# Constant products on an idle TensorE, and column sums spread among output tiles, in a two-block attention and Hyena kernel

## The reference, cut to what matters

```
def adaln_params(cond, w, b):
    mod = jax.nn.silu(cond) @ w + b
    return jnp.split(mod[..., None, :], 6, axis=-1)
...
    x = x + merged @ w_out                     # end of the first block
    x = rms_norm(x, norm_final)
...
    sh1, sc1, g1, sh2, sc2, g2 = adaln_params(c, mod_w, mod_b)
    h = modulate(rmsnorm(x, norm_g[0]), sh1, sc1)
    x = x + g1 * hyena_mix(h, ...)
    x = x + g2 * conv_ffn(modulate(rmsnorm(x, norm_g[1]), sh2, sc2), ...)
    return rmsnorm(x, final_g)
```

## Time and profile before

| | us |
|---|---|
| median of 3 runs | 1089.21 |
| lowest, highest | 1088.16, 1089.78 |
| the profiled execution | 1089.59 |
| its span, first to last instruction | 1087.8 |
| TensorE busy in the span | 1050.8 (97%) |
| VectorE, ScalarE, GpSimd busy | 666.7, 421.2, 543.9 |
| mean granted TensorE clock | 0.988 |

### The profile page before, as it was taken

How to read it: one execution, slowest core, us unless ns; L and a number is a source line. 1 busy time by engine, 2 the same in 40 slices (tenths; PEclk the granted TensorE clock), 3 DMA queues, 4 the chain that set the end, 5 groups by cost and what they waited for, 6 DMA issues and landing times.

```text
span 1087.8 us, 13471 instructions
## 1 busy us (share of the span) xinstructions
PE 1050.8 (97%) x4970; PEld 866.0 (80%) x4970; DVE 666.7 (61%) x1003; ACT 421.2 (39%) x691; POOL 543.9 (50%) x403
## 2 busy tenths in 40 slices
PE   6999998999899999999999999989999999999996
PEld 5889886877777888778888888868888888888885
DVE  5663667775478864966588864467656665620503
ACT  6223656574455243564344333333223322321222
POOL 1688789987000045343344346435546554663541
PEclk9999999999899999989999999999999999999999
DMA  6446354341344842230222223222232223222322
GB/s 250 159 164 226 123 189 168 99 152 44 143 160 176 347 172 67 95 116 14 104 77 78 79 78 155 78 97 78 97 136 77 77 96 136 77 78 99 134 78 77
DMA packets 18567, 131.92 MB, mean 121 GB/s; under 512 B 2369, under 2 KB 2769, under 8 KB 11986
## 3 DMA queue, kind: packets, MB, share of 16 engines
q1 hardware_dynamic: 8784, 92.62, 22.7%
q0 software_dynamic: 6560, 27.27, 7.4%
q10 hardware_dynamic: 3170, 11.30, 2.7%
HBM read 124.89 MB, written 6.29 MB: 121 GB/s over the span
## 4 chain that ended last, share of the span: by engine, by line
PE 85%; DVE 9%; ACT 3%; issue 1%; POOL 1%; DMA 1%; SPq 0%; POOLq 0%; ACTq 0%; DVEq 0%
PE bank L497 73%; PE bank L488 6%; PE bank L503 2%; PE bank L727 1%; PE bank L733 1%; DVE arena L2261 1%; DVE bank L2264 1%; DMA x_sb<-x_in 1%; ACT ring_parts L1143 1%; DVE arena L2101 1%; DVE arena L2319 0%; DVE arena L2104 0%; DVE arena L2317 0%; PE bank L722 0%; ACT arena L1143 0%
## 5 line engine op out<-in xcount | busy, mean ns | idle before, releaser
L1660 POOL TENSOR_TENSOR ring_parts<-ring,ring_parts 128x1024 fp32r<-128x1024 f32 x104 | 253.0, 2437 | 289.2 <-ACT ring_parts L1143 286.9
L1143 ACT ACTIVATE ring_parts<-ring 128x1024 fp32r<-128x1024 f32 (+2 forms) x163 | 168.7, 1042 | 471.4 <-PE bank L497 293.2
L497 PE MATMUL bank<-hT_parts,ring_parts 128*128 128x512 f32 x1344 | 341.9, 396 | 1.3 <-ACT hT_parts L1457 1.3
L497 PEld LDWEIGHTS bank<-hT_parts,ring_parts 128*128 128x128 f32 x1344 | 251.7, 190 | 55.9 <-ACT hT_parts L1457 3.0
L497 PE MATMUL bank<-ring_parts,arena_parts 128*128 128x512 f32 (+1 forms) x736 | 172.5, 387 | 1.5 <-DVE arena L2319 0.8
L497 PE MATMUL bank<-ring_parts,hT_parts 128*128 128x512 f32 (+1 forms) x672 | 171.7, 383 | 0.7 <-POOL ring_parts L1660 0.6
L497 PEld LDWEIGHTS bank<-ring_parts,arena_parts 128*128 128x128 f32 x736 | 136.5, 188 | 29.6 <-DVE arena L2319 1.3
L497 PE MATMUL bank<-arena_parts,ring_parts 128*128 128x512 f32 x592 | 147.8, 391 | 0.3 <-DVE arena_parts L2203 0.3
L497 PEld LDWEIGHTS bank<-ring_parts,hT_parts 128*128 128x128 f32 x672 | 123.8, 190 | 22.9 <-POOL ring_parts L1660 1.0
L2417 DVE SCALAR_TENSOR_TENSOR arena<-bank,small,arena 128x441 f32<-128x441 f32 (+2 forms) x176 | 122.3, 695 | 24.6 <-DVE arena L2412 1.9
L497 PEld LDWEIGHTS bank<-arena_parts,ring_parts 128*128 128x128 f32 x592 | 111.1, 188 | 25.5 <-DVE arena_parts L2203 2.1
(11 more groups left out here) (228 smaller groups left out, 1078.7 us busy)
## 6 DMA issues: line engine op xcount, KB each, us to landing
ring<-weights_in SPq DMA_DIRECT2D x39, 2048.0 KB, 7.9
arena<-mod_w_in POOLq DMA_DIRECT2D x32, 512.0 KB, 4.1
arena<-mod_w_in POOLq DMA_DIRECT2D x8, 1024.0 KB, 5.0
x_sb<-x_in SPq DMA_DIRECT2D x4, 512.0 KB, 5.6
ring<-weights_in SPq DMA_DIRECT2D x4, 512.0 KB, 8.5
mod_spill<-mod_part POOLq DMA_DIRECT2D x16, 128.0 KB, 2.1
x_sb<-x_in ACTq DMA_DIRECT2D x4, 512.0 KB, 12.1
arena<-mod_spill ACTq DMA_DIRECT2D x1, 2048.0 KB, 10.4
```

The costliest lines, as they stand in the source:

```text
L497: ins = nc.tensor.matmul(out, l, r, start=start and n == 0, stop=stop and n == len(passes) - 1)
L1143: return nc.scalar.activation(out, in_, ACT.Copy)
L1660: return nc.gpsimd.tensor_tensor(part(low), low, part(high), ALU.subtract)
```

## The change

`keep_running` is a plain fp32 product of the identity with the first n columns of `small`, whose result nobody reads. It is issued three times before the first token tile and once before the third; in the third norm after the turns of tiles 1 and 2 (512 columns each, in bank 0, after a wait for the reader of that bank) and once with 256 columns after the last turn of k = 1. `modulation(j)` now makes 4 column sums and runs eight times among the output and filter tiles; the gate products have a function of their own, and its last two use banks 4 and 5. VectorE's `modulation()` stands before `norm_x2(2)` instead of at the end, and ScalarE's `modg_copy(2)` after `square_x1(3)`.

```diff
+        MODG_BANK = (2, 2, 4, 5)
...
+            def keep_running(b, n=512):
+                nc.tensor.matmul(bank[b][:, 0:n], ident, small[:, 0:n], start=True, stop=True)
+
             pe.wait_ge(sem("small_in"), 16)
+            for _ in range(3):
+                keep_running(7)
             for m in range(TT):
+                if m == 2:
+                    keep_running(7)
                 pe.wait_ge(sem("n1_scaled"), m + 1)
...
-                for c in range(j * KD, (j + 1) * KD):
+                for c in range(4 * j, 4 * j + 4):
                     ins = nc.tensor.matmul(bank[3][:, c:c + 1], mod_sum(c), st(ONE), start=True, stop=True)
-                ins.then_inc(sem("modc_done"), 1)
-                take(2, "modg_out", j + 1)
-                nc.tensor.matmul(bank[2], ones_sq, mod_g[:, j // 2, (j % 2) * 512:(j % 2) * 512 + 512],
+                if j % 2:
+                    ins.then_inc(sem("modc_done"), 1)
+
+            def gate_rows(j):
+                b = MODG_BANK[j]
+                take(b, "modg_out", j + 1)
+                nc.tensor.matmul(bank[b], ones_sq, mod_g[:, j // 2, (j % 2) * 512:(j % 2) * 512 + 512],
                                  start=True, stop=True).then_inc(sem("modg_done"), 1)
...
             modulation(0)
+            gate_rows(0)
+            modulation(1)
             wo_tile(0)
+            modulation(2)
             wo_tile(1)
-            modulation(1)
+            gate_rows(1)
+            modulation(3)
             filter_tile(0)
             wo_tile(2)
+            modulation(4)
             filter_tile(1)
             wo_tile(3)
+            modulation(5)
             filter_tile(2)
             filter_tile(3)
             wo_tile(4)
+            modulation(6)
             filter_tile(4)
             wo_tile(5)
             abs_norm(0)
+            modulation(7)
             filter_tile(5)
             wo_tile(6)
             filter_tile(6)
             filter_tile(7)
             wo_tile(7)
-            modulation(2)
-            modulation(3)
+            gate_rows(2)
+            gate_rows(3)
...
                             turn(b, [x_norm[:, m, j * P:(j + 1) * P]], m)
+                        if m == 1:
+                            pe.wait_ge(sem("hyo_out"), TT + 1)
+                        if m:
+                            keep_running(0)
                     pe.wait_ge(sem("n3_scaled"), TT)
                 m = TT - 1
                 turn(N3_BANKS[k], [x_norm[:, m, k * P:(k + 1) * P]], m).then_inc(sem("n3_turned"), 1)
+                if k == 1:
+                    keep_running(0, 256)
...
             split_high(FIRST_HYZ)
+            square_x1(TT - 1)
             modg_copy(2)
-            square_x1(TT - 1)
             modg_copy(3)
...
             scale_n2(1)
+            modulation()
             norm_x2(2)
...
             scale_n2(3)
-            modulation()
```

More of the change, by code:

```diff
@@ L1397, in modg_copy @@
                 wait("modg_done", j + 1)
-                copy(mod_g[:, j // 2, (j % 2) * 512:(j % 2) * 512 + 512], bank[2]).then_inc(sem("modg_out"), 1)
+                copy(mod_g[:, j // 2, (j % 2) * 512:(j % 2) * 512 + 512], bank[MODG_BANK[j]]).then_inc(sem("modg_out"), 1)
             def square_x1(m):
```

## The result

The changed kernel takes 1092.56 us (median of nine runs, 1090.92 to 1093.15), the kernel before 1089.23 beside it: ratio 1.0027, 95% interval 1.0017 to 1.0037. It is slower by 3.3 us where 1.7 less were forecast. The profiled execution has a span of 1091.0 (before: 1087.8), so its own difference is 3.2. "Worth" and "cost" are what the shift moves by over a stretch.

What follows compares the result with a forecast made beforehand. TensorE was taken to bound the kernel (85% of the chain), VectorE setting the pace near 465. Terms -1.6 - 1.3 + 0.84 + 0.4 = -1.66 gave 1087.5 us against 1089.21, range 1084.5 to 1090.3.

Steps and rivals of the forecast that it cites:

- The begin, -1.6: Program start: constants' products raise TensorE's clock sooner, so the products of k=2 start at 16.75 instead of 18.35; -1.6 us.
- The third norm, -1.3: Third norm: constants fit into TensorE's gaps and keep the clock up, k=3 at 718.17 instead of 719.50; -1.3 us.
- So VectorE comes out of this 0.84 late: Output and filter tiles: sums delay GpSimd's pieces, so VectorE's chain runs late until 465; +0.84 us, bounds 0 and 1.68.
- the swallowing of the rest: Before `filter_tile(2)`: half of the 1.68 us of `modulation(4)` and `(5)` is swallowed, as VectorE's additions end with GpSimd's subtractions.
- Those that stood before `filter_tile(0)` still do: Output tiles: column sums and gate products ahead of the first filter tile stay ahead of it; no delay was counted there.
- Both places are on one chain [...], so nothing is won: Second norm: moving VectorE's `modulation()` (0.38 us) ahead of `norm_x2(2)` stays on one chain of norm, square, root, scale; 0.
- The clock, +0.4: Behind the second norm: the early spectrum leaves TensorE thin, the clock falls at 476.5 to 478 for 3.4 us; +0.4 us.
- the rival that had 1.5 in 10: The low clock moves behind the second norm and lasts, costing 2.1 instead of 0.4; 1089.2 us, 1.5 in 10.
- two signs of being wrong: First output tile to the turn of k=2 in the second norm gets shorter, or the stream's first products start after 14.7.
- The rival "slower": Begin: constants hold up the first tile if the clock rises later than 14; 1092.0 us, 0.8 in 10.

Runs made afterwards that it cites:

- e1: The kernel before with only the constants' products at the begin and in the third norm, nothing of the modulation's change; 3.6 us faster.
- e16: The kernel before with the constants alone, run again on another chip for a second profile; 1086.35 us, 0.9971 of the kernel before.
- e7: The changed kernel with only the second gate product moved, to behind the first tap tile; 1090.76 us.
- e5: The changed kernel with GpSimd's first split behind the second norm waiting until VectorE has scaled the last token tile; 1087.81 us.
- e2: The changed kernel without any constants' product, only the modulation's moves kept; 7.8 us slower than the kernel before.
- e9: The changed kernel itself once more, for a second profile; ratio 1.0008 to the kernel before.
- e6: The changed kernel with TensorE's order up to the third tap tile as before, plus GpSimd's wait for the last tile's scaling; 1090.4 us.
- e10: The changed kernel with both mends (late sums, GpSimd's extra wait) and two constants' products (512 and 256 columns) in the second norm; 1089.26 us.
- e12: The changed kernel with both mends (late sums, GpSimd's extra wait) once more, for a second profile; 1090.0 us.
- e14: The changed kernel with both mends (late sums, GpSimd's extra wait) again, beside the runs with the spectrum held back; 1089.7 us.
- e3: The changed kernel with VectorE's combining of the column sums back behind its scaling of the last token tile; 1088.06 us.
- e13: The changed kernel with both mends (late sums, GpSimd's extra wait) and the first taps' spectrum held until ScalarE squared the last token tile; 1090.2 us.
- e15: The changed kernel with GpSimd's extra wait and the first taps' spectrum held back, column sums left where the change puts them; 1089.5 us.
- e11: The changed kernel with constants' products in the second norm: three of 512 columns before the transposes, one of 256 after those of k=1; 1088.96 us.
- the mended kernel: The changed kernel with TensorE's earlier order up to the third tap tile and GpSimd's wait for the last tile's scaling; 1090.4, 1090.0 and 1089.7 us.

## Why the prediction was wrong

*The begin, -1.6:* right, -2.07; between -1.4 and -2.2 in the profiles of all kernels with the constants. The rise was taken 5.25 after the landing and came sooner, by the third constant. *The third norm, -1.3:* right, -1.33 (-1.30 in e1 and in e16).

*"So VectorE comes out of this 0.84 late":* mis-sized, 1.65. The 0.84 for the sums ahead of GpSimd's pieces measured 1.0 with the gaps beside them, and the swallowing of the rest is as forecast. But "Those that stood before `filter_tile(0)` still do" overlooked the second gate product's wait for bank 2 and ScalarE's copy, 0.65 (e7).

*"Both places are on one chain [...], so nothing is won":* the step that failed. It priced the instruction that moved, and for that it was right: in e5 the combining delays by 0.38 and gives it back. It didn't ask who waits for `modc_ready`. GpSimd does, its 2.34 us subtraction then started 0.13 ahead of VectorE's scaling, and that took 2.77 instead of 0.76: 2.0, and e5 won them back. The same contention had been read off the additions at 434 and 437 and used for the delay, but not looked for at the place that the change releases. The Trainium skill, "SBUF — State Buffer", section "SBUF: two separate sides", calls the port pair of VectorE and GpSimd an exclusive lock that is held for a whole instruction; by it the scaling waits from 473.00 to GpSimd's end at 475.21 and then does its work, until about 475.97. The trace agrees within 0.2: it ends at 475.77.

*The clock, +0.4:* a fall behind the second norm was forecast, and where; it lasted 6.8, as in the rival that had 1.5 in 10, and cost 1.4, between the forecast and that rival's 2.1. It goes with the stretched scaling, which left TensorE idle for 3.23 before the transposes (in e2 and e9, where the spectrum ran at the low clock, for 1.6): all six profiles that have it and no constants there show 6.8 us of low clock in this place, costing 0.45 to 1.9. Of the eight in which the sums are moved and the scaling is not stretched, the four mended ones (e6, e10, e12, e14) show 3.4 and the other four (e3, e5, e13, e15) none, and in e11, where the idle time is filled, there is none either. Why the mended ones keep 3.4 isn't shown. The Trainium skill, "TensorE: Matmul & The Clock Gate", section "Why this matters for your kernels", advises against gaps between bursts of matmuls; the full clock that the change won at 465 was worth nothing (with it the shift goes from -3.76 at 411 to -3.75 at 475 in e6), and the gap moved to where TensorE sets the pace.

*Near 530, +1.6:* in no step. Ten of the fifteen profiles with moved sums show it, none of the three without (before, e1, e16). Its cause stays open. It comes behind the eight one-column products of the tap norms, but these stand in all profiles; it isn't the early spectrum alone (e15), and it is missing in the changed kernel's own second profile. How much of the medians it carries isn't known either, since only one execution of each kernel is profiled. Nor is it shown why the mended kernel, with no wait left, stays 3.3 us behind the constants alone (medians of e14 and e16). Their profiled executions, 1088.11 and 1086.49, differ by 1.6 only: e14 loses 1.3 and 1.6 on two low stretches that e16 doesn't have there and is 1.35 ahead of it at 405, by the clock before 325. What lets the clock fall in just these places in most executions of the mended kernel is not settled.

The prediction named two signs of being wrong, a shorter stretch between the first output tile and the turn of k=2, and late first products. Neither came. That stretch was to get 0.8 longer and got 3.7 longer, for which it had no sign.

The rival "slower" was at the begin, the wrong place; the loss came where the prediction said that nothing changes.

## What to carry to other kernels

When an instruction is moved earlier, list who waits for its semaphore, and look at what each of them then runs beside: an early release let GpSimd stretch a VectorE instruction on the chain that mattered by 2 us. Price a low clock only where TensorE sets the pace: constants in its idle time at the begin and in the third norm gave 2.9 to 3.6 us, the full clock won beside VectorE's chain gave nothing and left a gap in a worse place. After mending every wait, measure again, since the clock may take back what the waits gave.

## What the runs showed of the hardware

A 128x1024 scaling on VectorE took 0.75 to 0.76 us when GpSimd's 2.3 us subtraction of the same size started behind it, and 2.77 or 2.78 us when that started 0.13 us ahead. The profile shows no wait there, only the longer instruction. Low stretches of TensorE's clock inside the kernels lasted 3.4 or 6.8 us. In all eighteen profiles each of them began at a gap of TensorE or within 2.1 us behind one, or else among or just behind one-column products (near 530, at 439.91 in e13, at 465.06 in the kernel before), on which the profile shows TensorE busy without a gap. Their places differ between two profiles of one kernel. In the changed kernel and in the mended one the times go with the mean granted clock: in e9 1087.4 to 1088.8 us at 0.995, 1092.9 to 1093.2 at 0.988 or 0.989. In the kernel before they do not: at a mean of 0.988 its times reach from 1087.93 to 1092.04 on one chip.
